# Second block of a two-block transformer on one core: source halves in turn, bias from shifted rows of memory, other banks for the keys, smaller first loads

## What is computed

```python
def rmsnorm(x, g): return x * rsqrt(mean(x*x, -1) + EPS) * g

def second_block(x, ...):                      # h: 512 x 1024
    h = x + gla_mixer(rmsnorm(h, ln_mix[0]), ...)          # ends with @ a_w_out      (stage go)
    h = h + mlp(rmsnorm(h, ln_mlp[0]), w_up, w_down)       # relu(..)**2, width 4096  (stage mlp0)
    k, v = split(rmsnorm(h, kv_norm) @ w_kv)               # 2 kv heads of 64         (stages sk, sv)
    q = rmsnorm(h, ln_mix[1]) @ b_w_q                      # 16 heads of 64           (stage sq)
    # sliding window of 128; bias[head, dist] from a table of 32 buckets; sink logits
    s = q k^T / 8 + bias[bucket(dist)]  (masked);  p = softmax with sink;  o = p v
    h = h + o @ b_w_out                                    #                          (stage so)
    h = h + mlp(rmsnorm(h, ln_mlp[1]), ...)                #                          (stage mlp1)
    return rmsnorm(h, ln_final)
```

## Time and profile before

| | |
|---|---|
| three executions | 2538.17, 2538.72, 2543.44 us, median 2538.72 |
| the profiled execution | 2538.33 us; its span in the profile 2536.6 us |
| busy share of PE (matmul), DVE, ACT | 97%, 58%, 34% |
| chain that ended last | PE 86%, DVE 8%, ACT 4%, nothing seen 1% |
| data moved by DMA | 226.09 MB, 89 GB/s over the span |

### The profile page before, as it was taken

How to read it: one execution, slowest core, us unless ns; L and a number is a source line. 1 busy time by engine, 2 the same in 40 slices (tenths; PEclk the granted TensorE clock), 3 DMA queues, 4 the chain that set the end, 5 groups by cost and what they waited for, 6 DMA issues and landing times.

```text
span 2536.6 us, 28955 instructions
## 1 busy us (share of the span) xinstructions
PE 2458.0 (97%) x11338; PEld 1998.7 (79%) x11338; DVE 1466.8 (58%) x2020; ACT 870.9 (34%) x1153; POOL 10.0 (0%) x23
## 2 busy tenths in 40 slices
PE   8999999999999999999998999999999999999998
PEld 7888777888887776888886787788888777788886
DVE  6888735544446735444446535556666665566666
ACT  3344533422223733322224434322222464322222
POOL 0000000000000000000000000000000000000000
PEclk9999999999999999999999999999999999999999
DMA  5222222222222211222222221232222211222221
GB/s 191 83 84 84 92 84 77 100 91 98 99 99 88 79 67 67 100 95 89 98 99 72 85 98 34 69 133 99 97 87 97 83 51 67 83 99 97 87 97 67
DMA packets 32924, 226.09 MB, mean 89 GB/s; under 512 B 3765, under 2 KB 3797, under 8 KB 6480
## 3 DMA queue, kind: packets, MB, share of 16 engines
q1 hardware_dynamic: 31536, 220.21, 25.2%
q0 software_dynamic: 1312, 4.81, 0.6%
HBM read 222.89 MB, written 2.12 MB: 89 GB/s over the span
## 4 chain that ended last, share of the span: by engine, by line
PE 86%; DVE 8%; ACT 4%; issue 1%; DMA 0%; DVEq 0%; ACTq 0%
PE bank L668 86%; DVE w_lo L1837 2%; ACT w_hi L1319 1%; ACT xs L1386 1%; DVE xs L1939 1%; ACT xh L1332 1%; DVE cacc L2052 1%; DVE hs L2103 0%; DVE xs L1956 0%; PE bank L1264 0%; DVE gs L2103 0%; DVE xl L1845 0%; DVE sum_x L1852 0%; DVE sum_q L1859 0%; DVE xs L1911 0%
## 5 line engine op out<-in xcount | busy, mean ns | idle before, releaser
L668 PE MATMUL bank<-xh,w_hi 128*128 128x512 f32 x1960 | 776.3, 396 | 38.7 <-DVE xl L1846 13.1
L668 PE MATMUL bank<-xl,w_hi 128*128 128x512 f32 x1960 | 767.1, 391 | 0.0
L668 PE MATMUL bank<-xh,w_lo 128*128 128x512 f32 x1960 | 766.8, 391 | 0.0
L1837 DVE TENSOR_TENSOR w_lo<-w_raw,w_hi 128x2048 fp32r<-128x2048 f32 x205 | 469.7, 2291 | 399.0 <-ACT w_hi L1319 398.5
L1319 ACT ACTIVATE w_hi<-w_raw 128x2048 fp32r<-128x2048 f32 x205 | 391.5, 1910 | 396.9 <-PE bank L668 396.8
L668 PEld LDWEIGHTS bank<-xh,w_hi 128*128 128x128 f32 x1960 | 370.9, 189 | 132.1 <-issue 27.9
L668 PEld LDWEIGHTS bank<-xl,w_hi 128*128 128x128 f32 x1960 | 370.8, 189 | 78.0 <-issue 2.5
L668 PEld LDWEIGHTS bank<-xh,w_lo 128*128 128x128 f32 x1960 | 370.4, 189 | 77.9
L1911 DVE TENSOR_TENSOR xs<-xs,bank 128x512 f32<-128x512 f32 x448 | 294.7, 684 | 115.8 <-PE bank L668 114.6
L668 PE MATMUL bank<-mhh,w_lo 128*128 128x512 f32 x512 | 199.2, 389 | 0.0
L668 PE MATMUL bank<-mhh,w_hi 128*128 128x512 f32 x512 | 199.2, 389 | 0.0
(11 more groups left out here) (265 smaller groups left out, 2509.9 us busy)
## 6 DMA issues: line engine op xcount, KB each, us to landing
w_raw<-weights_in SPq DMA_DIRECT2D x205, 1024.0 KB, 4.9
xs<-x_in SPq DMA_DIRECT2D x4, 512.0 KB, 6.5
sf<-rel_scratch POOLq DMA_DIRECT2D x1, 2048.0 KB, 11.7
y_out<-xs SPq DMA_DIRECT2D x8, 256.0 KB, 2.0
w_raw<-weights_in SPq DMA_DIRECT2D x2, 512.0 KB, 5.5
mk<-mem_in POOLq DMA_DIRECT2D x1, 1024.0 KB, 8.2
window<-consts_in POOLq DMA_DIRECT2D x1, 576.0 KB, 6.1
sum_q<-consts_in POOLq DMA_DIRECT2D x1, 256.0 KB, 8.3
```

The source lines that it names most:

```text
L668: return pe.matmul(dst, a, b, start=start, stop=stop)
L1837: dve.tensor_tensor(w_lo[:, c % 2, :], w_raw[:, c % 2, :], w_hi[:, c % 2, :].bitcast(F32), ALU.subtract)\
```

## The change

- (a) The first two tiles of x and the two quarters of the first half unit are loaded and split one by one, alternately.
- (b), (f) `residual` makes the gained halves of a pair of tiles right behind its sum, in `yh`/`yl`; mlp0 and mlp1 read those, go and so read `xh`/`xl`.
- (c) The first up of an MLP uses banks 0 and 1, all others 2 and 3.
- (d) `vec` is multiplied at k-tile 4 of mlp0's first unit and stored negated in `vt`. POOL writes each row of `vt` 128 times to memory (eight DMAs of two heads, 256 x 384) and reads with a step of 383 (eight DMAs of 128 x 2 x 256) straight to `bias`, one DMA per unit of mlp0. The flip, its matmuls and drains are gone.
- (e) With the last down ACT and DVE make the `kvn` halves in `xh`/`xl`; sk takes banks 4 and 5. Then come the `mix2_g1` halves in `yh`/`yl`, then the squares and their sums. PE's three sum matmuls move from k-tile 3 of sk to k-tile 3 of sq's first unit. ACT waits for the bias ahead of the drain of `vt`, DVE ahead of the first scores.

The diff, cut:

```diff
@@ plan_banks
-        b = 2 if gated else 0
+        b = 2 if gated else 2 * ((UNITS[name] + (tag != "first")) % 2)
...
-    for m in range(2):
-        fill(("bias", m), 4 + m % 2)
+    fill(("sk", 0, 0), 4)
+    fill(("sk", 0, 1), 5, UNITS["sk"])
     norm("r2", False)
-    pairs("sk", 1)
-    for m in range(2, 8):
-        fill(("bias", m), 4 + m % 2)
@@ SyncE
-            sp.dma_start(xs[:, 0:2, :], x[:, 0:2, :]).then_inc(x_loaded[0], 16)
             half = UNIT // 2
-            sp.dma_start(w_raw[:, 0, 0:half], w[0, :, 0:half]).then_inc(first_half_loaded, 16)
-            sp.dma_start(xs[:, 2:4, :], x[:, 2:4, :]).then_inc(x_loaded[1], 16)
+            for k in range(2):
+                a = slice(k * half // 2, (k + 1) * half // 2)
+                sp.dma_start(xs[:, k, :], x[:, k, :]).then_inc(x_loaded[k], 16)
+                sp.dma_start(w_raw[:, 0, a], w[0, :, a]).then_inc(first_quarter_loaded[k], 16)
+            sp.dma_start(xs[:, 2:4, :], x[:, 2:4, :]).then_inc(x_loaded[2], 16)
@@ POOL
-            pool.dma_start(scratch, vt[0:16, 0:384]).then_inc(vec_stored, 16)
-            pool.wait_ge(vec_stored, 16)
-
-            hankel = bass.AP(tensor=scratch.tensor, offset=0, ap=[[1, P], [384, 16], [1, 2 * P]])
-            pool.dma_start(sf[:, :].rearrange("p (h k) -> p h k", h=16), hankel).then_inc(hankel_loaded, 16)
+            for g in range(8):
+                heads = slice(2 * g, 2 * g + 2)
+                pool.wait_ge(unit_used, UNITS["mlp0"] + 4 + g)
+                pool.dma_start(scratch[heads, :, :], vt[heads, 0:384].unsqueeze(1).broadcast_to([2, P, 384])).then_inc(vec_stored, 16)
+            pool.wait_ge(vec_stored, 8 * 16)
+            for g in range(8):
+                pool.wait_ge(unit_used, UNITS["mlp0"] + 14 + g)
+                shifted = bass.AP(tensor=scratch.tensor, offset=2 * g * P * 384 + 127, ap=[[383, P], [P * 384, 2], [1, 2 * P]])
+                pool.dma_start(bias[:, 2 * g:2 * g + 2, :], shifted).then_inc(bias_loaded, 16)
@@ TensorE
+                src = xtile if gate else ytile
...
-                    if k == 2:
+                    if k == behind:
                         rms_norm_sums(name)
+                    if name == "r1" and k == behind + 2:
+                        relative_values()
...
-            bias_tile(0)
-            bias_tile(1)
-            ytile = lambda k: (yh[:, k, :], yl[:, k, :])
-            feature_unit("sk", 0, ytile, ready=kv_ready)
-            for m in range(2, 8):
-                bias_tile(m)
+            feature_unit("sk", 0, ready=tile_ready)
...
-            feature_unit("sq", 0, ready=tile_ready)
+            feature_unit("sq", 0, ytile, ready=tile_and_sums("r2", 3))
@@ ScalarE
                         wait_drained(act, keys[k])
-                        if k == KT - 1 and gain:
-                            late_high(gain, keys[k], range(1))
+                        if gain:
+                            high(k, xs[:, k, :], col(gain, k), yh)
                         square(k, xs[:, k, :])
-                if gain:
-                    late_high(gain, keys[KT - 1], range(1, KT))
...
+            split_hi(UNITS["sk"] + 1)
             for k in range(KT):
-                high(k, xs[:, k, :], col("kvn", k), yh)
+                high(k, xs[:, k, :], col("mix2_g1", k), yh)
+            split_hi(UNITS["sv"] + 1)
+            for k in range(KT):
+                square(k, xs[:, k, :])
             rms_stats("r2")
@@ VectorE
+                    for k in (2 * j, 2 * j + 1) if gain else ():
+                        give(rest(k, xs[:, k, :], col(gain, k), yh, yl), "tile_ready")
...
                     add(k, keys[k])
-                    sums_between(k, keys, has_mean)
-                split_lo(c + 1)
+                    if name == "mlp0":
+                        if k == 1:
+                            split_lo(c + 1)
+                        if k:
+                            wait_drained(dve, keys[k - 1])
+                            give(rest(k - 1, xs[:, k - 1, :], col("kvn", k - 1)), "tile_ready")
+                    else:
+                        sums_between(k, keys, has_mean)
```

More of the change, by code:

```diff
@@ L975, in up @@
                             for m in range(2):
-                                last = mm3(bank((name, tag, which, m))[:, :], weights(c, k * 256 + m * P, P), xtile(k),
+                                last = mm3(bank((name, tag, which, m))[:, :], weights(c, k * 256 + m * P, P), src(k),
                                            k == 0, k == KT - 1)
@@ L1205, in _ @@
             for k in range(KT):
[L1206 removed]
+                last = mm3(bank(("sv", 0, 0))[:, :], weights(c, k * P, P), xtile(k), k == 0, k == KT - 1)
             full(last, ("sv", 0, 0))
@@ L1575, in cross_attention @@
                 return step
-            act.wait_ge(x_loaded[0], 16)
             for k in range(2):
+                a = slice(k * UNIT // 4, (k + 1) * UNIT // 4)
+                act.wait_ge(x_loaded[k], 16)
                 high(k, xs[:, k, :])
-            for half in range(2):
-                a = slice(half * UNIT // 2, (half + 1) * UNIT // 2)
-                act.wait_ge(raw_loaded[0] if half else first_half_loaded, 16)
-                act.activation(w_hi[:, 0, a], w_raw[:, 0, a], ACT.Copy).then_inc(w_hi_ready if half else sem["first_hi"], 1)
-                for k in range(2 + 2 * half, 4 + 4 * half):
-                    if k % 2 == 0:
-                        act.wait_ge(x_loaded[k // 2], 16)
-                    high(k, xs[:, k, :])
+                act.wait_ge(first_quarter_loaded[k], 16)
+                give(act.activation(w_hi[:, 0, a], w_raw[:, 0, a], ACT.Copy), "first_hi")
+            act.wait_ge(x_loaded[2], 16)
+            for k in range(2, 4):
+                high(k, xs[:, k, :])
+            act.wait_ge(raw_loaded[0], 16)
+            act.activation(w_hi[:, 0, UNIT // 2:], w_raw[:, 0, UNIT // 2:], ACT.Copy).then_inc(w_hi_ready, 1)
+            for k in range(4, KT):
+                if k % 2 == 0:
+                    act.wait_ge(x_loaded[k // 2 + 1], 16)
+                high(k, xs[:, k, :])
             seen.next("lbd_ready")
@@ L1760, in _ @@
             chunks("mlp0")
-            wait_full(act, ("mlp0", "last", "d", KT - 1))
+            split_hi(UNITS["sk"] + 1)
             for k in range(KT):
-                high(k, xs[:, k, :], col("kvn", k), yh)
-            def drain_bias(m):
-                key = ("bias", m)
-                drain(key, bias[:, 2 * m:2 * m + 2, :], bank(key)[:, :].rearrange("p (h k) -> p h k", h=2), scale=-1.0)
-            drain_bias(0)
-            drain_bias(1)
-            rms_stats("r2")
-            high(0, xs[:, 0, :], col("mix2_g1", 0))
-            high(1, xs[:, 1, :], col("mix2_g1", 1))
-            split_hi(UNITS["sk"] + 1)
-            for k in range(2, KT):
-                drain_bias(k)
-                high(k, xs[:, k, :], col("mix2_g1", k))
-            split_hi(UNITS["sv"] + 1)
+                high(k, xs[:, k, :], col("mix2_g1", k), yh)
+            split_hi(UNITS["sv"] + 1)
+            for k in range(KT):
+                square(k, xs[:, k, :])
+            rms_stats("r2")
             def swa(it):
@@ L1888, in xs_at, with residual @@
                 return xs[:, k, :]
-            def residual(keys, c0, n_units, has_mean, alpha=None, first=0):
+            def residual(keys, c0, n_units, has_mean, alpha=None, first=0, gain=None):
                 for j in range(n_units):
@@ L1977, in scale_residual @@
                 steps.wait()
-            def late_rest(gain, l):
-                for k in range(KT):
-                    give(rest(k, xs[:, k, :], col(f"{gain}_g{l}", k)), "tile_ready")
             def chunks(name, has_mean):
@@ L2204, in cross_attention, with first_rest @@
                 return step
+            def first_rest(a):
+                return dve.tensor_tensor(w_lo[:, 0, a], w_raw[:, 0, a], w_hi[:, 0, a].bitcast(F32), ALU.subtract)
             for k in range(2):
                 give(rest(k, xs[:, k, :]), "tile_ready")
-            for half, ready in ((slice(0, UNIT // 2), "first_lo"), (slice(UNIT // 2, UNIT), None)):
-                if ready:
-                    seen.next("first_hi")
-                else:
-                    dve.wait_ge(w_hi_ready, 1)
-                dve.tensor_tensor(w_lo[:, 0, half], w_raw[:, 0, half], w_hi[:, 0, half].bitcast(F32), ALU.subtract)\
-                   .then_inc(sem[ready] if ready else w_lo_ready, 1)
-                if ready:
-                    for k in range(2, 4):
-                        give(rest(k, xs[:, k, :]), "tile_ready")
+                seen.next("first_hi")
+                give(first_rest(slice(k * UNIT // 4, (k + 1) * UNIT // 4)), "first_lo")
+            for k in range(2, 4):
+                give(rest(k, xs[:, k, :]), "tile_ready")
+            dve.wait_ge(w_hi_ready, 1)
+            first_rest(slice(UNIT // 2, UNIT)).then_inc(w_lo_ready, 1)
             for k in range(4, KT):
@@ L2425, in _ @@
```

(6 more changed lines are left out.)

89 lines of the change are left out of this document (39 added, 50 removed).

## The result

Five executions of the changed kernel took 2522.62 to 2529.18 us, median **2528.56**; beside it the kernel before had 2538.72. The ratio is 0.9947 [0.9935, 0.9959]: faster by 10.2 us, where 23.2 were forecast, and above the range. The profiled execution took 2529.02 us.

What follows compares the result with a forecast made beforehand. TensorE, busy 97% of the span, was taken as the bound. Gains of 2.2 + 3.6 + 12.2 + 4.9 = 22.9 us off the profiled 2538.33 gave 2515.5 us, range 2511.5 to 2523.

Steps and rivals of the forecast that it cites:

- the cost of the bias by DMA: In mlp0: each replicating write takes about 2 to 4 us, each read about 2, so PE loses nothing.
- Rival 3: In mlp0: replicated writes on few engines hold the weights, 17.5 us per write; 2549 to 2595 us, slower; chance 0.04.
- rival 4: A mild hold-up of weights by the writes, or an unseen wait, takes the gain back: 2534 to 2543 us; chance 0.03.
- rivals 1 and 2: Gains come in part, 2517 to 2520 us, chance 0.14; ACT and DVE late in the middle, 2518 to 2521, 0.09.
- The start: First loads: smaller pieces let PE start at about 5.75 instead of 8.02; gain taken as 2.2 us.
- go to mlp0: From go to mlp0's start: PE's waits for the one-hot matrix and the first up's drain both go; gain 3.6 us.
- so to mlp1: From so to mlp1: the gap, slow clock and wait at the second up go; gain 4.9 us, bounds 3.4 to 5.0.
- The banks' share: Second up of mlp0 and mlp1: PE's wait for the first up's drain goes; 1.04 and 0.95 us.
- The middle: From mlp0's last down to the queries: waits, clock dip and flips go; gain 12.2 us, the largest term.
- the late split with its dip: Ahead of the keys: two flips and a wait, 3.90 us, and the clock dip behind the gap, 1.72, go.
- the flips: Between keys and values: six flips on PE go; 5.56 us.
- rival 2: Middle: ACT and DVE run late, so the queries wait for weights or squares; 2518 to 2521 us; chance 0.09.

Runs made afterwards that it cites:

- E1: Changed kernel with each replicating write turned to all 16 heads and 16 of the 128 copies, instead of two heads and all copies: 2520.34 us, ratio 0.9924.
- E2: Changed kernel with the same two-head writes issued every second unit of mlp0 instead of every unit, reads later: 2521.06 us, ratio 0.9918.
- E3: Kernel before with only the eight two-head writes added, into memory that nothing reads: 2542.46 us, ratio 1.0013.
- E8: E1 with 14 fp32 128 x 128 matmuls on ones ahead of the first unit, results unused: 2519.81 us, ratio 0.9924.
- E9: E1 with the first loads, splits and waits of the kernel before, plus 14 fp32 matmuls on ones ahead of the first unit: 2517.51 us, ratio 0.9908.
- E5: E1 with all ups of mlp0 and mlp1 in banks 0 and 1 again: 2518.85 us, ratio 0.992.
- E6: E1 with the keys' unit split behind the last rest again: 2525.02 us, ratio 0.9946.
- E7: E1 with six more fp32 128 x 512 matmuls behind the keys, results unused: 2524.69 us, ratio 0.9942.

## Why the prediction was wrong

- **The step that failed** is the cost of the bias by DMA: "A write of 256 such runs over 16 engines is then about 2 to 4 us ... So nothing". It took the 16 engines of the row of `sf`, a DMA of 128 partitions, for one whose outer dimension is two. Measured: about 20 us per write, on about two engines, loads of up to 21.9 beside them, and 6.6 and 6.0 us lost in the two profiles. E1 takes it away by the shape alone, E2 by the spacing alone, and E3 brings it without the rest. By time the writes' shape is worth 8.2 of the 13.1 us that are missing (2528.56 against the 2520.34 of E1). That two-head writes hold the weights is shown; whether by their two engines, their two source partitions or their packets is not.
- **Rival 3 had the mechanism and a wrong price.** Its 17.5 us per write was close to the 20, its sum was not: it let all eight units wait for a whole write, and put the point where the kernel becomes slower than before at 10.4 us per write. At 20 it was still 10.2 us faster. Loads slowed down to 10.5 to 21.9 but did not wait for the writes in turn; the two buffers covered up to about 17.8, and PE stopped once. My argument against it, that a load at most trebles its 4.9 and stays inside 17.5, failed too: with two writes under way it took 4.5 times as long. Given 0.04 and rival 4 another 0.03, the pair was too cheap for a step without a row, whose engine count the cited rule gave as two. The 2528.56 lies between the times of rivals 1 and 2 and that of rival 4, in none of them.
- **The start** was forecast at 2.2 and is worth about 1.3. Tile 0 landed at 3.77 (3.7 forecast), but the first quarter at 5.58 instead of 4.45, 1.8 behind it and not 0.75 (1.3 to 1.8 in the eight profiles with new loads). The formula taken there from the Trainium skill (DMA: Bandwidth & Descriptors, Anatomy of one DMA) is fitted to single DMAs that GpSimd issues; these are several in a row from SyncE. Then most of the earlier start was spent at the low clock, which lasted to about 12 us in both kernels. The forecast counted PE's first matmul as the gain, without counting what follows it at 0.43 apiece. E8 and E9 bear this out.
- **go to mlp0** 3.6 (3.6 forecast), **so to mlp1** 5.2 (4.9): right. The banks' share is 1.1 at each (1.04 and 0.95 forecast, E5). At so to mlp1 no dip came, as expected without a gap.
- **The middle** 11.9 (12.2): right. Two of its parts were tested: E6 gives 6.2 for the late split with its dip (3.90 + 1.72), E7 5.2 for the flips (5.56). The queries came 16.66 after the last down instead of 16.3, and neither their rests nor their squares were waited for, so rival 2 didn't occur.
- **The rest** of the first profile's miss is mostly clock: 3.3 ahead of go and 1.3 at the end of attention. Both occur in the kernel before as well, in some executions. Without the two-head writes the forecast of 22.9 would have stood against the 20.1 of E1 in the ledger, and 2515.5 against 2520.34: still 5 too low, but in the range. So the range would have held by its width, with the start 1.5 short of its term in that profile and 1.3 lost to a dip that the forecast didn't have.

## What to carry to other kernels

Look at the outermost dimension of a DMA before calling it hidden: one of two rows by 128 copies used about two engines, and beside such DMAs loads of another queue took up to 21.9 us instead of 4.8; turn it so that the outer dimension is 16, or keep such DMAs apart. The page's median landing hides this, so ask for minimum and maximum in the stretch where the new DMA runs. Don't read the length of a DMA from its landing where several count on one semaphore. An earlier first matmul is worth little while the clock is low and the data is late: look at when PE reaches its pace, not when it starts.
